# Plain slabs combined inside pairs 2 to 5 of the up-projection, and the first pair's order on DVE, ACT and SP rewritten

## What is computed

```python
h = rmsnorm(x, g_mlp[l])
x = x + jnp.square(jax.nn.relu(h @ w_up[l])) @ w_down[l]     # w_up 1024 x 4096, w_down 4096 x 1024
```

## Time and profile before

| | |
|---|---|
| time, median of 3 | 2525.82 us (2523.96 to 2527.11) |
| the profiled execution's own time | 2525.3 us |
| its span, first to last instruction | 2523.5 us |
| PE busy | 2388.8 us, 95% of the span |
| DVE busy | 1707.2 us, 68% |
| ACT busy | 1119.9 us, 44% |
| pairs of layer 0 | 639.35 to 948.19 us |
| pairs of layer 1 | 1878.28 to 2187.37 us |

### The profile page before, as it was taken

One profiled execution on the slowest core, in us unless ns is written; L12 is line 12 of the kernel. 1 busy time (PEld: TensorE's weight loads), 2 busy tenths in 40 slices (PEclk: granted clock), 3 DMA queues, 4 the chain that ended last, 5 costly groups with the idle time before them and its releaser, 6 DMA issues.

```text
span 2523.5 us, 32747 instructions
## 1 busy us (share of the span) xinstructions
PE 2388.8 (95%) x11857; PEld 1936.7 (77%) x11857; DVE 1707.2 (68%) x3130; ACT 1119.9 (44%) x1984; POOL 269.5 (11%) x287
## 2 busy tenths in 40 slices
PE   7999899899899989999999989998999999799997
PEld 6877777678788877888878777776777888688886
DVE  5555666666877768888636556666577777697873
ACT  5554444553444433333436544454454444333333
POOL 1111011123000000000221111121220000000003
PEclk9999999999999999999999999999999999899999
DMA  5201011211344467868331000102114444787753
GB/s 171 76 26 26 18 26 34 67 51 48 117 145 144 152 216 247 270 191 263 126 88 30 26 26 18 34 26 67 59 42 159 142 154 157 239 274 237 222 178 98
DMA packets 289928, 296.06 MB, mean 117 GB/s; under 512 B 19510, under 2 KB 236640, under 8 KB 289512
## 3 DMA queue, kind: packets, MB, share of 16 engines
q1 hardware_dynamic: 284056, 278.24, 35.0%
q10 hardware_dynamic: 5712, 15.73, 1.6%
HBM read 212.10 MB, written 81.82 MB: 116 GB/s over the span
## 4 chain that ended last, share of the span: by engine, by line
PE 78%; DVE 8%; issue 4%; ACT 4%; DMA 2%; DVEq 2%; POOL 0%; SPq 0%; ACTq 0%; POOLq 0%
PE ps L1883 23%; PE ps L2150 19%; PE ps L2202 8%; PE ps L2203 8%; PE ps L2204 8%; PE ps L2016 3%; PE ps L1963 3%; PE ps L2046 2%; PE ps L2036 1%; DVE probs L1393 1%; ACT probs L1018 1%; DVE probs L1421 1%; ACT pt_both L1036 1%; PE ps L2048 1%; DMA b_saved<-v_tile 1%
## 5 line engine op out<-in xcount | busy, mean ns | idle before, releaser
L2202 PE MATMUL ps<-b_hi,d_hi 128*128 128x512 f32 x896 | 350.7, 391 | 10.7 <-DVE d_lo L1685 10.6
L1883 PE MATMUL ps<-wide_hi,w_hi 128*128 128x512 f32 x1024 | 339.5, 413 | 21.2 <-POOL w_lo L871 6.3
L2204 PE MATMUL ps<-b_hi,d_lo 128*128 128x512 f32 x896 | 349.9, 391 | 0.0
L2203 PE MATMUL ps<-b_lo,d_hi 128*128 128x512 f32 x896 | 349.9, 391 | 0.0
L1883 PE MATMUL ps<-wide_lo,w_hi 128*128 128x512 f32 x1024 | 321.6, 396 | 0.0
L1883 PE MATMUL ps<-wide_hi,w_lo 128*128 128x512 f32 x1024 | 319.2, 393 | 0.0
L1444 DVE TENSOR_TENSOR pt_both<-ps,pt_both 128x512 fp32r<-128x512 f32 (+3 forms) x216 | 126.4, 585 | 222.8 <-ACT pt_both L1036 222.0
L1140 ACT ACTIVATE d_hi<-d_raw 128x1024 fp32r<-128x1024 f32 x112 | 118.4, 1058 | 338.3 <-DVE d_raw L1674 110.8
L1036 ACT ACTIVATE pt_both<-ps 128x512 fp32r<-128x512 f32 (+3 forms) x216 | 110.4, 511 | 337.6 <-PE ps L2016 337.3
L871 POOL TENSOR_TENSOR w_lo<-w_raw,w_hi 128x256 fp32r<-128x256 f32 x216 | 164.4, 792 | 830.2 <-ACT w_hi L921 830.2
L1018 ACT ACTIVATE probs<-probs,neg_max,slope 128x256 f32<-128x256 f32 (+7 forms) x256 | 202.3, 791 | 95.3 <-DVE neg_max L1408 75.2
(11 more groups left out here) (204 smaller groups left out, 4471.6 us busy)
## 6 DMA issues: line engine op xcount, KB each, us to landing
b_raw<-b_saved SPq DMA_DIRECT2D x112, 512.0 KB, 6.6
d_raw<-in_w_down_dram SPq DMA_DIRECT2D x112, 512.0 KB, 6.3
a_raw<-in_w_up_dram SPq DMA_DIRECT2D x60, 512.0 KB, 4.2
b_saved<-c_rows SPq DMA_DIRECT2D x120, 256.0 KB, 4.4
w_raw<-in_w_in_dram SPq DMA_DIRECT2D x92, 256.0 KB, 3.3
b_saved<-far SPq DMA_DIRECT2D x32, 512.0 KB, 4.2
w_raw<-in_w_out_dram SPq DMA_DIRECT2D x36, 256.0 KB, 3.0
x_saved<-xt ACTq DMA_DIRECT2D x16, 512.0 KB, 2.6
```

The source lines that it names most:

```text
L1883: mm = T.matmul(ps[p][:, bass.ts(t, BANK)], w, h[:, bass.ts(t, BANK)], start=(start and n == 0), stop=(stop and n == 2))
L2202: T.matmul(out, w0, b0, start=first, stop=False)
L2203: T.matmul(out, w0, b1, start=False, stop=False)
L2204: mm = T.matmul(out, w1, b0, start=False, stop=last)
```

## The change

It does four things. (1) The rings' squared halves are stored straight into `b_saved`, as 256 KB pieces. (2) The plain slabs' four combinations are made one by one in pairs 2 to 5: SP loads two pieces of 256 KB into `far`, DVE combines them in place, SP stores one piece. (3) The weight slot of P4 in pair 0 moves from `ring1`'s memory to that of `far` (`far_hi`, `far_lo`), and P4's slot waits for ring1's stores in pair 1. (4) The lists of DVE, ACT and SP for pair 0 and the way into pair 1 are written in another order. At the end of the pairs `load_plain`, `make_plain_t`, `store_plain` and `store_plain_t` are gone from all lists, and two `load_d` stand where `load_plain` stood.

```diff
+        def a_slot(l, n, i):
+            return (far_hi, far_lo) if (n, i) == (0, P4) else (a_hi[l][i], a_lo[l][i])
...
-            if n:
+            if (n, i) == (0, P4):
+                return
+            if (n, i) == (1, P4):
+                engine.wait_ge(ring_stored[1], 32 * (l + 1))
+            elif n:
                 engine.wait_ge(product, products(l, n - 1, i))
...
                         sp.wait_ge(a_split, products(l, n - 1, P6 if h == 0 else P4))
+                        if (n, h) == (1, 0):
+                            sp.wait_ge(a_summed, 4 * NP * l + 3)
...
-                    sp.dma_start(plain_saved[m], ring[m][:]).then_inc(ring_stored[m], 16)
+                    for dst, at in ((kept(P2 if m else P1, -1), 0), (kept(P3, -1) if m else plain_saved, H)):
+                        sp.dma_start(dst, ring[m][:, at:at + H]).then_inc(ring_stored[m], 16)
...
+                def load_plain(p, n):
+                    sp.wait_ge(t13_stored, 16 * (NP * l + n))
+                    if 4 * l + p:
+                        sp.wait_ge(v_stored, 16 * (4 * l + p))
...
+                    for src, at in ((first, 0), (second, H)):
+                        sp.dma_start(far[:, at:at + H], src).then_inc(v_loaded, 16)
+
+                def store_plain(p):
+                    sp.wait_ge(v_made, 4 * l + p + 1)
+                    sp.dma_start(kept((P5, P7, P6, P4)[p], -1), far[:, 0:H]).then_inc(v_stored, 16)
...
-                for m in range(NPLAIN):
-                    store_ring(m)
...
                 load_a(1, 0)
+                store_ring(0)
                 for n in range(NP - 1):
                     load_a(n + 1, 1)
-                    if n:
-                        store_t13(n - 1)
...
+                    if n == 0:
+                        store_ring(1)
+                        store_block(0, C11)
+                        store_block(0, C22)
+                        load_a(2, 0)
+                        continue
...
+                    if 2 <= n < 6:
+                        load_plain(n - 2, n)
                     if n + 2 < NP:
                         load_a(n + 2, 0)
+                    if 2 <= n < 6:
+                        store_plain(n - 2)
                     store_block(n, C11)
                     store_block(n, C22)
-                load_plain()
+                load_d(0, "A21")
+                load_d(1, "A11")
...
+                    if n == 0:
+                        dve.wait_ge(product, products(l, 0, P4))
                     V.tensor_tensor(far_t, c_pair[l], c_block[l][C12].unsqueeze(1).to_broadcast([P, 2, H]),
                                     ALU.subtract).then_inc(t13_made, 1)
...
+                def make_plain_t(p):
+                    dve.wait_ge(v_loaded, 32 * (4 * l + p + 1))
+                    V.tensor_tensor(far_t[:, 0], far_t[:, 0], far_t[:, 1], ALU.add if p == 2 else ALU.subtract).then_inc(v_made, 1)
...
+                add_block(0, C11)
+                add_block(0, C22)
                 a_low(0, P4)
-                for n in range(NP):
+                hidden(1)
+                a_low(1, P1)
...
+                sum_a(1, 0)
+                V.drain()
+                sum_a(1, 1)
+                a_low(1, P5)
+                rectify(0, C21)
+                make_t13(0)
+                make_t2(0)
+                sum_a(1, 2)
+                V.drain()
+                sum_a(1, 3)
+                for i in (P6, P2, P7, P3, P4):
+                    a_low(1, i)
...
-                    if not ahead:
-                        make_plain_t()
...
                     rectify(n, C11)
+                    if 2 <= n < 6:
+                        make_plain_t(n - 2)
```

More of the change, by code:

```diff
@@ L383, in hybrid_encoder @@
         ones = small("ones", [P, 1])
+        far_at = cursor[0]
         far = small("far", [P, S])
+        far_hi = place("far_hi", [P, NC // 2, P], far_at, F32R)
+        far_lo = place("far_lo", [P, NC // 2, P], far_at + 2 * KB, F32R)
         near = small("near", [P, 2 * P])
@@ L704, in load_d @@
                             sp.wait_ge(product, products(l, NP - 1, P5))
[L705 to L709, removed]
+                        elif t < 3:
+                            sp.wait_ge(a_split, products(l, NP - 1, P4))
                         else:
@@ L1178, in _ @@
                 a_high(0, P3)
+                a_high(0, P4)
                 copy_out(0, P6)
                 square_ring(1)
-                a_high(0, P4)
-                for n in range(NP - 1):
-                    if n:
-                        copy_out(n, P1)
+                a_high(1, P1)
+                square_block(0, C11)
+                square_block(0, C22)
+                square_block(0, C12)
+                a_high(1, P5)
+                square_block(0, C21)
+                for i in (P6, P2, P7, P3, P4):
+                    a_high(1, i)
+                for n in range(1, NP - 1):
+                    copy_out(n, P1)
                     a_high(n + 1, P1)
-                    if n:
-                        copy_out(n, P5)
-                        copy_out(n, P6)
+                    copy_out(n, P5)
+                    copy_out(n, P6)
                     a_high(n + 1, P5)
@@ L1738, in _ @@
                 sum_a(0, 2)
+                t_low(T3)
+                a_low(0, P7)
                 V.drain()
                 sum_a(0, 3)
-                t_low(T3)
-                a_low(0, P7)
-                hidden(1)
                 a_low(0, P3)
                 t_low(T4)
+                add_block(0, C11)
+                add_block(0, C22)
                 a_low(0, P4)
-                for n in range(NP):
+                hidden(1)
+                a_low(1, P1)
+                V.drain()
+                rectify(0, C11)
+                rectify(0, C22)
+                add_block(0, C12)
+                V.drain()
+                rectify(0, C12)
+                sum_a(1, 0)
+                V.drain()
+                sum_a(1, 1)
[4 more added lines that the diff above has]
+                sum_a(1, 2)
+                V.drain()
+                sum_a(1, 3)
+                for i in (P6, P2, P7, P3, P4):
+                    a_low(1, i)
+                for n in range(1, NP):
                     ahead = n + 1 < NP
-                    if n:
+                    if n > 1:
                         make_t13(n - 1)
                         make_t2(n - 1)
-                    if ahead and n:
+                    if ahead:
                         a_low(n + 1, P1)
@@ L1757, in _ @@
                         a_low(n + 1, P5)
-                    if n:
-                        V.drain()
-                        make_t4(n - 1)
-                    if not ahead:
-                        make_plain_t()
+                    V.drain()
+                    make_t4(n - 1)
                     add_block(n, C11)
-                    if ahead and n:
+                    if ahead:
                         sum_a(n + 1, 2)
                     V.drain()
-                    if ahead and n:
+                    if ahead:
                         sum_a(n + 1, 3)
                     rectify(n, C11)
-                    if ahead and n:
+                    if 2 <= n < 6:
+                        make_plain_t(n - 2)
+                    if ahead:
                         a_low(n + 1, P6)
                         a_low(n + 1, P2)
-                    elif not ahead:
+                    else:
                         d_low(0)
@@ L2147, in multiply @@
                     for c in range(NC // 2):
[L2148 removed]
+                        w0, w1 = [t[:, c] for t in a_slot(l, n, i)]
                         for k, (w, h) in enumerate(((w0, h_hi), (w0, h_lo), (w1, h_hi))):
```

85 lines of the change are left out of this document (20 added, 65 removed).

## The result

| | before | changed |
|---|---|---|
| median | 2525.99 us (2523.96 to 2527.11, 4 runs) | 2551.99 us (2546.05 to 2555.70, 4 runs) |
| ratio, 95% interval | | 1.0102 (1.0080 to 1.0123) |
| profiled execution, its span | 2525.3, 2523.5 us | 2546.05, 2544.3 us |
| mean granted clock of that execution | 0.984 | 0.982 |

The profiled execution of the changed kernel is the fastest of its four; the other three had 0.976 to 0.979 as mean clock. The spans differ by 20.8 us, the medians by 26.0. Against the forecast of +8 the sign and the three places were right and the size was not.

What follows compares the result with a forecast made beforehand. PE, busy for 95% of the span, was taken as the bound, with no slack to DVE's chain. Per layer 4.0 + 3.6 - 3.6 = +4.0, two layers +8.0: 2534 us against the median 2525.8, range 2517 to 2542.

Steps and rivals of the forecast that it cites:

- the three places: Pairs 2 to 5 (+4.0 us a layer), pair 0 and the way into pair 1 (+3.6), pair 14 and first units (-3.6).
- the middle: Pairs 2 to 5: the added operation's late loads start P4 1.0 us late in each of four pairs, +4.0 a layer.
- Pairs 2 to 5: Added operation behind C11's rectify starts 1.0 us late, waiting for its loads: +4.0 a layer, ends 0.9 and 6.0.
- 914.25: Pairs 2 to 5, on pair 13's timeline: time the two loads were taken to have landed; operation then starts 1.0 us late.
- the end of 1.5: Pairs 2 to 5: upper end of the cost a pair, 6.0 us a layer.
- the rival called faster: Loads of pairs 2 to 5 land in DVE's hole, ring0's stores in time too: -6 us, 2520; chance 0.2.
- idle stretches of 1 us at no clock: Pairs 2 to 5: TensorE's idle stretches of 1 us lower no clock, as P7 of pair 0 (0.86) ran full rate.
- First two pairs: Ring0's stores wait behind pair 1's load, delaying P7 of pair 0 and DVE's list: pair 2 starts +3.6 us a layer.
- 0.1 against 3.6: First two pairs, us a layer: +0.1 if ring0's stores land before P3's weight needs them, +3.6 if they wait.
- my +5.5 end: First two pairs: upper end, with one more slow start at P4 of pair 1, behind 2.9 us idle.
- Pair 14 and the units: Four DVE operations and a 5.10 us wait go, `d_low(0)` starts earlier: -3.6 us a layer, ends -4.5 and -2.8.
- The rival called worse: End gains less or more clock is lost: +5.5, +6 and -2.8 a layer make +17 us, 2543; chance 0.13.

Runs made afterwards that it cites:

- e9_loads_first: Changed kernel with SP issuing the plain combination's two loads ahead of T4's store, not behind it: median 2530.97 us, ratio to before 1.0016.
- e1_late: Changed kernel with the plain combination of pairs 2 to 5 behind C22's rectify instead of C11's: median 2529.83 us, ratio to before 1.0004.
- e2_ring_first: Changed kernel with SP issuing ring0's two stores ahead of pair 1's first weight half: median 2538.62 us, ratio to before 1.0042.
- e5_late_ring: Changed kernel with the edits of e1_late and e2_ring_first together: median 2523.75 us, ratio to before 0.9986.
- e10_t4_place: Changed kernel with the places in memory of T4 of pair 3 and of pair 4 exchanged: 2550.06 us in one run.
- e8_shift3: Changed kernel with the four plain combinations in pairs 3 to 6 instead of 2 to 5: 2553.21 us in one run.
- e6_lr_a1: e5_late_ring plus ACT making pair 1's first high part ahead of ring1's square: median 2520.45 us, ratio to before 0.9976.
- e7_lr_a1_copy: e6_lr_a1 plus ACT copying P1 of pair 1 behind P2's high part, not P4's: median 2518.22 us, ratio to before 0.9965.

## Why the prediction was off

The step that failed is the largest term, the middle: the landing of the two loads was priced too low, and in pair 5 the idle stretch that it leaves was taken to cost no clock. That is 8.2 us of the 12.8 by which the span missed. The first two pairs add another 2.8.

**Pairs 2 to 5, +4.0 a layer forecast, +8.1 measured.** The mechanism was right: no slack between DVE and TensorE, a hole of 0.62 that takes the operation (e9_loads_first), and a cost that is the loads' lateness alone (e1_late, e9_loads_first). The mis-sized term is the landing of the loads. In pairs 2 to 4 I took 914.25, which is 2.85 us behind the second issue; it was 3.4 (704.48 to 707.92), so a pair cost 1.45 and not 1.0. That is near the end of 1.5 that I had worked out from the weight loads. The value I took lay near the least of these loads (2.7) and not at their median (3.2), and in every pair of the changed kernel the second load was slower than that median. "The queue is empty at that time", the argument of the rival called faster, left out T4's own store, issued 0.4 us ahead of the first load. No run shows what the two loads take with nothing else in flight. The page's estimate that I set beside it (the Trainium skill, DMA: Bandwidth & Descriptors, Anatomy of one DMA) has both pieces there 3.2 us behind the first issue; here it was 3.85 in pair 2 and 4.57 in pair 5, so it was short as well. The section fits DMAs that GpSimd issues, and these are SP's. Pair 5 lay outside both ends: 3.7 us, of which some 2.2 are TensorE's wait and 1.4 its P4, mostly at 1.2 GHz (773.39 to the next pair's start at 777.68, 4.29 instead of 2.86). Where the clock held, in layer 1 of e2_ring_first, the same pair took 21.57, 2.3 over. I had costed idle stretches of 1 us at no clock; this one had grown to 2.20.

**First two pairs, +3.6 forecast, +5.0 and +5.1 measured.** Each step showed: P6 earlier, the load ahead of the stores, ACT waiting for ring0's store (to 653.43; forecast 652.8), P7 at 655.12 (654.5) with 3.98 us idle (3.9) and a slow start, DVE's list as the longer chain into pair 1. Undoing the order of the load and the stores gave 3.8 to 4.0 back, forecast as 0.1 against 3.6, so 3.5. The miss of 1.4 is at the chain's end. P7 is 0.3 later against the first product than forecast, and `make_t4` in pair 1, costed with no wait of its own, waits 0.86 for C21's store, which had been queued behind both halves of pair 2's weights and T13's store; the rest is a few tenths along the list. This split is layer 0's. In layer 1 `make_t4` starts as late, 44.2 us behind the first product, behind 0.51 us that no DMA ends; there the weights land later instead, so the store's part is not shown to be the cause:

```profile
683.86 0.69 DVE L1661 TENSOR_TENSOR c_rows<-c_rows,t_tile 128x512 f32<-128x512 f32 x1 [0.86 <-DMA b_saved<-c_rows]
```

P6 of pair 1 ran at the low clock after 2.57 us idle, where the kernel before had kept full clock after 2.52. In this kernel P4 was waiting for DVE anyway, so it added little; my +5.5 end had put the slow start at P4.

**Pair 14 and the units, -3.6 forecast, -4.4 and -2.4 measured.** The step held: `d_low(0)` stands 15.4 us behind pair 14's start (947.37 - 931.94; forecast 16.4, before 20.0) and 16.6 in layer 1, P4 still waits 3.1 (forecast 4) and the third unit 4.54.

```profile
947.37 1.23 DVE L1689 TENSOR_TENSOR d_lo<-d_raw,d_hi 128x1024 fp32r<-128x1024 f32 x1 [2.15 <-ACT d_hi L1145]
```

Up to the third unit it is -4.8 and -3.6; behind it both layers lose some again. Over both layers it is -6.7 for -7.2 forecast. The combined kernels bear it out as the gain that is left once the two costs are gone (-4.9 and -3.3 in e5_late_ring).

**What the terms don't hold.** The last stage was 2.3 longer in the profiled execution, and the medians differ by 5 us more than the profiled spans. The other executions had the same work at a mean clock of 0.976 to 0.979. With the waits of pairs 2 to 5 gone, the mean clock is 0.980 to 0.987 in e1_late and 0.979 to 0.985 in e9_loads_first, like the kernel before. So I read these 5 us as clock lost around the stalls, execution by execution, but none of the slower executions has a trace: argued, not shown. The rival called worse (2543, "more clock is lost") was the nearest, and it too stopped short: it gave every term its end once, and had no place for a pair dearer than its bounds. The stated range ended at 2542, below even that rival's own figure.

## What to carry to other kernels

Before an operation with a load in front is put into a list that has no slack, price the load by loads of its size in the trace, at their median or above it where a store is in flight ahead, not by a store, and count from the last of its pieces. Better, issue the load one step earlier in its queue, or put the operation behind the instruction that the bottleneck waits for: either cost one moved line here and gave back the middle's whole cost. A wait that has once been hidden can be moved whole; one that grows from 1.4 to 2.2 us may cost the clock on top. Ask of every store what stands ahead of it in the queue and what first needs its landing.

## What was unexpected in the hardware

- Two 256 KB loads from DRAM were issued just behind a 256 KB store. The first landed 2.5 to 3.3 us behind its issue and the second 3.0 to 3.9, but 3.8 to 4.0 and 4.1 to 4.5 when the store went to one certain place in DRAM. It was the same in both layers of every kernel and moved with the place when two were exchanged (e10_t4_place). The store itself then took 2.4 to 2.6 us, which stores to two other places did as well, and 2.0 in pair 5 with the loads 4 us ahead of it (e9_loads_first). There the loads took 3.6 and 4.4 us, behind another store to the same place of its row.
- Nearly equal idle stretches of TensorE (2.52 us in the kernel before, 2.57 in the changed one) ended once at full clock and once at the low one. In the up-projections of all runs, stretches of up to 1.9 us left the clock at 2.4 GHz, but for one of 1.91 (pair 6 of layer 1 in e8_shift3). From 2.1 us on most ended at 1.2 GHz and some did not: 2.23 in e2_ring_first, 2.41 in e6_lr_a1, 2.90 in e7_lr_a1_copy.
